# Differential attention: the second map scaled by the ratio of the sums, squared sums in the heads' norm, and another order at its end

## The reference, cut to what matters

```python
def block(qi):
    s = jnp.einsum('bqhcd,bkhcd->bhcqk', qi, k).astype(jnp.float32) * scale
    p = jax.nn.softmax(s, axis=-1)
    a = (p[:, :, 0] - lam_full * p[:, :, 1]).astype(v.dtype)
    return jnp.einsum('bhqk,bkhd->bqhd', a, v)
...
o = rms_norm(o, subln_g) * (1.0 - lambda_init)   # per head, NORM_EPS = 1e-6
return o.reshape(B, S, H * dv) @ w_o
```

## Time and profile before

| | us |
|---|---|
| median of 3 runs | 1878.87 |
| their range | 1876.99 to 1879.66 |
| the profiled execution | 1877.12 |
| its span in the trace | 1875.3 |
| first to last scores of the attention (steps 2 to 31) | 150.53 to 238.48 |

### The profile page before, as it was taken

The page is one execution under the profiler, slowest core; times in us unless marked ns, Lnnn a source line. Parts: engine busy times, 40 slices in busy tenths (PEclk is TensorE's granted clock), DMA queues, the critical chain, the costliest instruction groups (busy, mean ns, idle before and its releaser), DMA issues.

```text
span 1875.3 us, 28169 instructions
## 1 busy us (share of the span) xinstructions
PE 1845.4 (98%) x10762; PEld 1587.3 (85%) x10762; DVE 1155.8 (62%) x1647; ACT 816.0 (44%) x1433; POOL 379.4 (20%) x303
## 2 busy tenths in 40 slices
PE   9999999999999999999999999999999999999997
PEld 7885578889889899998889888897888898989897
DVE  6967956644787557677642366625474368857474
ACT  5226855434546354552123522226553455535361
POOL 0430006500032315104310033300200000522311
PEclk9999999999999999999999999999999999999999
DMA  4330014402233332423331122320451123233331
GB/s 167 124 101 23 1 56 145 147 12 91 79 102 108 95 101 90 124 68 90 92 112 56 46 90 91 99 70 30 140 180 57 58 79 103 78 115 101 99 113 45
DMA packets 99059, 167.73 MB, mean 89 GB/s; under 512 B 5632, under 2 KB 32384, under 8 KB 98688
## 3 DMA queue, kind: packets, MB, share of 16 engines
q1 hardware_dynamic: 98944, 166.15, 27.8%
HBM read 164.03 MB, written 2.10 MB: 89 GB/s over the span
## 4 chain that ended last, share of the span: by engine, by line
PE 88%; DVE 5%; ACT 3%; issue 2%; DMA 1%; SPq 0%; POOL 0%; DVEq 0%; ACTq 0%; POOLq 0%
PE ps L1953 60%; PE ps L1993 10%; PE ps L2022 6%; PE ps L2115 2%; PE ps L2302 2%; PE ps L2310 1%; PE ps L2240 1%; PE ps L2176 1%; PE ps L2170 1%; DVE small L1591 1%; DVE w_lo L1267 1%; PE ps L2249 1%; PE ps L2255 1%; PE ps L2236 1%; PE ps L2048 1%
## 5 line engine op out<-in xcount | busy, mean ns | idle before, releaser
L1267 DVE TENSOR_TENSOR w_lo<-raw,w_hi 128x1024 fp32r<-128x1024 f32 x256 | 332.5, 1322 | 238.5 <-ACT w_hi L752 236.9
L752 ACT ACTIVATE w_hi<-raw 128x1024 fp32r<-128x1024 f32 x256 | 264.6, 1057 | 345.0 <-PE ps L1953 333.5
L1953 PE MATMUL ps<-act_hi,w_lo 128*128 128x512 f32 x860 | 340.8, 396 | 2.1 <-DVE act_lo L1418 1.7
L1953 PE MATMUL ps<-act_lo,w_hi 128*128 128x512 f32 x864 | 336.7, 390 | 0.0
L1953 PE MATMUL ps<-act_hi,w_hi 128*128 128x512 f32 x860 | 335.6, 390 | 0.0
L1953 PEld LDWEIGHTS ps<-act_hi,w_lo 128*128 128x128 f32 x860 | 161.8, 188 | 39.4 <-issue 2.8
L1953 PEld LDWEIGHTS ps<-act_lo,w_hi 128*128 128x128 f32 x864 | 162.7, 188 | 34.9 <-issue 1.9
L1953 PEld LDWEIGHTS ps<-act_hi,w_hi 128*128 128x128 f32 x860 | 161.9, 188 | 34.1
L1953 PE MATMUL ps<-ff_hi,w_hi 128*128 128x512 f32 x448 | 174.4, 389 | 0.0
L1953 PE MATMUL ps<-ff_lo,w_hi 128*128 128x512 f32 x448 | 174.4, 389 | 0.0
L1953 PE MATMUL ps<-ff_hi,w_lo 128*128 128x512 f32 x448 | 174.4, 389 | 0.0
(11 more groups left out here) (252 smaller groups left out, 4043.2 us busy)
## 6 DMA issues: line engine op xcount, KB each, us to landing
raw<-in_db_w_qkv SPq DMA_DIRECT2D x72, 512.0 KB, 3.8
raw<-in_w_up SPq DMA_DIRECT2D x64, 512.0 KB, 3.8
raw<-in_w_down SPq DMA_DIRECT2D x64, 512.0 KB, 3.7
raw<-in_xa_wkv SPq DMA_DIRECT2D x32, 512.0 KB, 3.8
raw<-in_da_w_qkv SPq DMA_DIRECT2D x24, 512.0 KB, 3.9
raw<-in_xa_wq SPq DMA_DIRECT2D x16, 512.0 KB, 3.8
raw<-in_xa_wo SPq DMA_DIRECT2D x16, 512.0 KB, 3.6
raw<-in_da_w_o SPq DMA_DIRECT2D x8, 512.0 KB, 3.6
```

The lines of the kernel that those rows point to most:

```text
L752: nc.scalar.activation(w_hi[:, g % 4], raw[:, g % 4], ACT.Copy).then_inc(w_hi_ready, 1)
L1267: nc.vector.tensor_tensor(w_lo[:, g % 4], raw[:, g % 4], w_hi[:, g % 4].bitcast(f32), ALU.subtract).then_inc(w_lo_ready, 1)
L1953: last = nc.tensor.matmul(ps[:, s + m, 0:width], left, right, start=(k == 0 and n == 0 and not early), stop=(k == KT - 1 and n == 2))
```

## The change

It rewrites the weights as e1 - lambda (s1/s2) e2: the first map isn't divided. What was a pass of 128 x 512 on DVE (L1617) becomes one of 128 x 1. Each row of a head's output is then s1 times what it was, so the epsilon of the norm has to be multiplied by s1 squared: ACT writes diag(s1) squared for each step (`squared_sum`, a square of the identity matrix scaled by s1, 128 x 128), and PE adds all-ones times that, 128 x 512, to each head's statistic. Preparing pair 1 of o0 moves from steps 8 and 9 to the attention's end, pairs 2 and 3 move there too, the low parts of heads 2 to 5 are made there, and PE's pair 0 of o0 moves ahead by two transposes, a product and a statistic; the last head's statistic moves behind pair 1.

```diff
@@ scalar engine, attention()
                             nc.scalar.activation(a.p[:, n % 2, 0:a.blocks * P], a.turned_all(n),
                                                  ACT.Copy).then_inc(a.pT, 1)
+                    if a is att_d and 1 <= t <= a.n:
+                        squared_sum(a, t - 1)
...
+            def squared_sum(a, t):
+                h, s = divmod(t, a.steps)
+                if h >= 2 and s == 0:
+                    act.wait_ge(sub_stat, h - 1)
+                act.wait_ge(a.exps, 2 * t + 1)
+                nc.scalar.activation(sums_sb[:, h % 2, s * P:(s + 1) * P], ident[:, :], ACT.Square,
+                                     scale=small[:, t % 2, 4:5]).then_inc(sum_squared, 1)
+
+            def last_pairs(u):
+                def event(a, h):
+                    if h == a.heads - 1:
+                        for j in range(1, 4):
+                            heads_of(4 * u + j)
+                return event
...
             def exp_diff(a, t):
+                if t >= 2:
+                    act.wait_ge(sum_squared, t - 1)
...
-            attention(att_d, exp_diff, 2, (2, diff_out), (4, second_pair(UNITS["o0"])), (5, diff_root), (7, diff_head))
+            attention(att_d, exp_diff, 2, (2, diff_out), (5, diff_root), (7, diff_head), (-1, last_pairs(UNITS["o0"])))
...
@@ vector engine; LATE_RESTS = ((), (2, 3), (4, 5), ())
+            def last_pairs(u, heads):
+                def event(h):
+                    if h == heads - 1:
+                        for j in range(1, 4):
+                            for k in LATE_RESTS[j]:
+                                head_rest(k)
+                            rests_of(4 * u + j)
+                return event
...
-                mid(nc.vector.reciprocal(s[:, 6:8], s[:, 4:6]))
-                mid(nc.vector.tensor_scalar(e[:, S:2 * S], e[:, S:2 * S], s[:, 7:8], lam_w[:, 5:6], ALU.mult, ALU.mult))
-                nc.vector.scalar_tensor_tensor(e[:, 0:S], e[:, 0:S], s[:, 6:7], e[:, S:2 * S], ALU.mult,
+                mid(nc.vector.reciprocal(s[:, 7:8], s[:, 5:6]))
+                mid(nc.vector.tensor_scalar(s[:, 6:7], s[:, 7:8], s[:, 4:5], lam_w[:, 5:6], ALU.mult, ALU.mult))
+                nc.vector.scalar_tensor_tensor(e[:, 0:S], e[:, S:2 * S], s[:, 6:7], e[:, 0:S], ALU.mult,
                                                ALU.add).then_inc(a.probs, 1)
...
-            attention(att_d, take_max, probs_diff, range(2, att_d.n + 9), (5, second_pair(UNITS["o0"])), (6, diff_scale), (8, diff_rest))
+            attention(att_d, take_max, probs_diff, range(2, att_d.n + 9), (6, diff_scale), (8, diff_rest), (0, last_pairs(UNITS["o0"], DA_HEADS)))
...
@@ tensor engine
-                nc.tensor.matmul(ps[:, att_d.out_bank(h), :], ones[:, :], stage[:, h % 2, :], start=True,
-                                 stop=True).then_inc(sub_stat, 1)
+                pe.wait_ge(sum_squared, att_d.steps * (h + 1))
+                bank = ps[:, att_d.out_bank(h), :]
+                nc.tensor.matmul(bank, ones[:, :], stage[:, h % 2, :], start=True, stop=False)
+                nc.tensor.matmul(bank, ones[:, :], sums_sb[:, h % 2, :], start=False, stop=True).then_inc(sub_stat, 1)
...
-            attention(range(2, att_d.n + 1), *diff)
-            pe.wait_ge(att_d.exps, 2 * att_d.n)
-
-            def mixer_ends():
-                attention(range(att_d.n + 1, att_d.n + 5), *diff)
+            attention(range(2, att_d.n), *diff)
+            pe.wait_ge(att_d.exps, 2 * (att_d.n - 1))
+
+            def last_scores_read():
+                pe.wait_ge(att_d.exps, 2 * att_d.n)
+
+            def diff_ends():
+                attention(range(att_d.n, att_d.n + 4), *diff)
+
+            def last_head_stat():
+                attention(range(att_d.n + 4, att_d.n + 5), *diff)
...
+                    unit(o, act_hi, act_lo, split, late_banks=last_scores_read,
+                         before_pair={1: diff_ends, 2: last_head_stat})
```

More of the change, by code:

```diff
@@ L143 @@
 LINE_PAD = 176
+LATE_RESTS = ((), (2, 3), (4, 5), ())
 REGION = 9 * KT * 256
@@ L245, in build @@
         posf = sb("posf", [P, S])
+        with ExitStack() as scope:
+            sums_sb = sb("sums_sb", [P, 2, S], scope=scope)
         mask = sb("mask", [P, DIL, S], bf16)
@@ L360, in build @@
         sub_sq = sem("sub_sq")
+        sum_squared = sem("sum_squared")
         sub_stat = sem("sub_stat")
@@ L835, in unit, with copies @@
                         between(2 + m // 2)
-            def copies(u, dst, nb=4, width=NB, scale=None, squares_at=None, between=None, second=2, first_steps=None):
+            def copies(u, dst, nb=4, width=NB, scale=None, squares_at=None, between=None, second=2, first_steps=None, done=2):
                 def bank(m):
@@ L845, in bank @@
                                          ).then_inc(bank_out[u % 2], 4 // nb)
-                unit(u, bank, nb=nb, between=between, second=second, first_steps=first_steps)
+                unit(u, bank, nb=nb, between=between, done=done, second=second, first_steps=first_steps)
             def root(name, dst=rstd):
@@ L1032, in diff_out @@
                     act.wait_ge(sub_stat, h - 1)
-                nc.scalar.activation(stage[:, h % 2, :], ps[:, att_d.out_bank(h), :], ACT.Square).then_inc(sub_sq, 1)
+                nc.scalar.activation(stage[:, h % 2, :], ps[:, att_d.out_bank(h), :], ACT.Square,
+                                     scale=(P * EPS) ** -0.5).then_inc(sub_sq, 1)
                 nc.scalar.activation(y_sb[:, h, :], ps[:, att_d.out_bank(h), :], ACT.Copy).then_inc(a.o_out, 1)
@@ L1040, in diff_root @@
                     act.wait_ge(sub_y, h - 1)
-                nc.scalar.activation(half[:, h % 2, :], ps[:, att_d.out_bank(h), :], ACT.Ln, bias=eps[:, 0:1],
-                                     scale=1.0 / P).then_inc(sub_ln, 1)
+                nc.scalar.activation(half[:, h % 2, :], ps[:, att_d.out_bank(h), :], ACT.Ln,
+                                     scale=EPS).then_inc(sub_ln, 1)
                 act.wait_ge(sub_ln, h + 1)
@@ L1129, in mem_heads @@
                             staged_head(f"mem{layer}", k, mem_hi, MEM)
-                copies(u, lambda m: y_sb[:, m, :], squares_at=0, between=first_mem_heads)
+                copies(u, lambda m: y_sb[:, m, :], squares_at=0, between=first_mem_heads, done=2 if layer else 4)
                 copies(u + 1, lambda m: y_sb[:, 4 + m, :], squares_at=4, between=mem_heads)
@@ L1678, in diff_rest, with head_rest @@
             def diff_rest(h):
+                if h not in LATE_RESTS[1] + LATE_RESTS[2]:
+                    head_rest(h)
+            def head_rest(h):
                 rest("o0", h, act_lo[:, h, :], act_hi[:, h, :], y_sb[:, h, :])
-            attention(att_d, take_max, probs_diff, range(2, att_d.n + 9), (5, second_pair(UNITS["o0"])), (6, diff_scale), (8, diff_rest))
+            attention(att_d, take_max, probs_diff, range(2, att_d.n + 9), (6, diff_scale), (8, diff_rest), (0, last_pairs(UNITS["o0"], DA_HEADS)))
             def by_token(ap):
@@ L1741, in mem_rests @@
                         mem_tile(layer, KT)
-                unit(u, between=first_mem_rests)
+                unit(u, between=first_mem_rests, done=2 if layer else 4)
                 unit(u + 1, between=mem_rests)
@@ L2283, in _ @@
                 split = SPLITS[f"o{layer}"]
-                unit(o, act_hi, act_lo, split,
-                     before_pair={1: mixer_ends})
+                if layer == 0:
+                    unit(o, act_hi, act_lo, split, late_banks=last_scores_read,
+                         before_pair={1: diff_ends, 2: last_head_stat})
+                else:
+                    unit(o, act_hi, act_lo, split,
+                         before_pair={1: mixer_ends})
                 unit(o + 1, act_hi, act_lo, split)
```

## The result

The changed kernel is slower: 1884.38 us in the median of 7 runs (1882.85 to 1886.40) against 1878.87 of the kernel before in the same comparison, a ratio of 1.0031 with a 95% interval of 1.0021 to 1.0040. The forecast was +7.1 us; the medians differ by 5.5, the ratio says 5.8. The profiled execution took 1884.65 us, its span 1882.9.

What follows compares the result with a forecast made beforehand. A circle of waits through ACT and PE, not DVE, was taken to set the 12.24 us head period; +7.16 up to step 31's scores and -0.08 at the end gave +7.1 us, 1886.0, range 1881.0 to 1889.5.

Steps and rivals of the forecast that it cites:

- The circle through ACT and PE: Layer 0's attention: spacings between waiting instructions on ACT and PE sum to 12.24 us, the whole period of one head.
- The first rival: Attention heads: DVE is the limiter, a head would take 12.0 us, -2.4 us in all, 1876.5; chance 0.12.
- The hiding squares: Rival in the attention: ACT's squares fall into waits, circle 13.10, +3.7 us in all, 1882.6; chance 0.13.
- the dearer ones: Rival: squares at 0.40 us each add 1.4, grouped with a dearer statistic or late end, 1888.7 to 1889.5; chance 0.11.
- The circle after: One attention head after the change: 12.24 + 0.86 for PE's second product + 2 x 0.28 for squares = 13.66 us.
- 7.16 forecast: Delay of the scores of step 31: 5.16 for statistics + 3.08 for squares - 1.08 for the moved pair, in us.
- Pair 1 of o0: Steps 8 to 13 of the attention: moving its preparation out of steps 8 and 9 gives 1.08 us.
- The end: After the scores of step 31: waits -2.33, statistics +1.72, one square +0.28, number format +0.25, sum -0.08 us.
- The two statistics: Attention's end: statistics of heads 6 and 7 grow by 2 x 0.86 = 1.72 us.
- the two waits: Attention's end: step 32's transposes wait 1.06 us, the last statistic 1.27; both go, -2.33 us.
- change of number format: Attention's end: one more change between fp32 and fp32r products on PE, allowed 0.25 us, an estimate.
- pair 0 of o0+1: Behind o0: the next thing to be late, with 1.5 to 2 us of cover left before PE needs it.

Runs made afterwards that it cites:

- e5_small_pass: Kernel before with DVE's pass of 128 x 512 taken away and nothing added, old norm, no squared sums: ratio 0.9997 to the kernel before.
- e6_large_pass: Changed kernel with DVE's pass given back its size, 128 x 512 instead of 128 x 1: ratio 1.0030 to the kernel before.
- e3_no_squares: Changed kernel without ACT's squared sums, PE adding a matrix of unrelated numbers: ratio 1.0016 to the kernel before, a head 13.01 us.
- e2_maths_alone: Kernel before with the new arithmetic alone (ratio of sums, squared sums, second product), its end untouched: ratio 1.0048 to the kernel before.
- e1_end_alone: Changed kernel with the old arithmetic put back, keeping only the new order of the end: ratio 0.9975 to the kernel before.
- e4_no_product: Changed kernel without PE's second product per statistic, ACT still squaring the sums: ratio 0.9997 to the kernel before, a head 12.72 us.
- e7_gpsimd_adds: Changed kernel with squares and their addition made by GpSimd and the head's output copied by DVE: ratio 0.9977 to the kernel before.

## Why the prediction was right, point by point

*The bound.* The circle through ACT and PE held. It adds up to the whole period in both kernels, and four kernels moved it by what their edit has in it: 0.01 and 0.00 for DVE's pass taken away and given back, 0.56 for the squares, 0.85 for the product. The first rival, DVE as the limiter, fell with `e5_small_pass` and `e6_large_pass`: the head is 13.57 with either size of the pass, where that rival wanted 12.0 for the changed kernel, and stays at 12.24 when the kernel before loses the pass, where it wanted 11.7 or less. The hiding squares fell with `e3_no_squares`, the dearer ones with the spacing of 0.29.

*The circle after: 13.66 forecast, 13.57 measured.* A square cost 0.29 for 0.28, the product 0.86 for 0.86. What the sum missed is the root: the change drops the logarithm's bias, and its spacing to the exponential falls from 0.73 (212.76 to 213.49 in the trace of before) to 0.63 (231.72 to 232.35 above). I read the edit as one of numbers only. Of the 0.38 us between 7.16 forecast and 6.78 measured at the scores of step 31, 0.31 lies in the four heads from step 13 to 29 and comes of this, less the squares' 0.01.

*Pair 1 of o0: 1.08 forecast.* The kernel with the new end alone shows 1.08. In the changed kernel 18.39 us from step 8 to 13 stand against a forecast of 16.97 + 1.48 = 18.45. The sum holds there, its terms don't stand by themselves: with the new arithmetic in place the move is worth 0.17, as `e2_maths_alone` shows, and the arithmetic costs 1.59 us in these five steps with pair 1 in them (16.97 to 18.56), 2.50 without (15.89 to 18.39).

*The end: -0.08 forecast, -1.08 measured.* This is the term that was mis-sized. The two statistics were right: the changed kernel's end is 1.91 longer than that of the new end alone, forecast 2.0 (1.72 for the statistics, the square 0.19 instead of 0.28). The reordering was not: I took the two waits at their shown 1.06 and 1.27 and allowed 0.25 for a change of number format, -2.08 together; the new end alone shows 28.35 - 31.34 = -2.99. The waits that a row shows are less than what goes with them. Between the product at 240.46 and the transposes at 242.68 lie 2.22 us, though the product without a wait behind it takes 0.89 (247.70 to 248.59 above), so 1.33 went where the row said 1.06. Between the last products at 251.05 and the statistic at 254.33 lie 3.28, though those products take 1.77 without the wait (249.89 to 251.66 with the new end alone), so 1.51 went where the row said 1.27. The transposes behind the first wait stood 0.58 from the product, without it 0.44: 0.14 more. That is 2.98 of the 2.99. What is left, a further change of number format among it, adds up to nothing; no run shows the 0.25. PE at the end of the changed kernel, to hold beside the earlier trace rows:

```profile
254.89 0.60 PE L2154 MATMUL ps<-ident,e_sb 128*128 128x128 f32 x4
255.33 1.06 PE L2215 MATMUL ps<-pT_sb,v 128*128 128x128 f32 x8
256.22 1.02 PE L2225 MATMUL ps<-stage,ones 128*128 128x512 f32 x2
257.08 1.02 PE L2226 MATMUL ps<-sums_sb,ones 128*128 128x512 f32 x2
257.94 0.60 PE L2154 MATMUL ps<-ident,e_sb 128*128 128x128 f32 x4
...
265.72 1.02 PE L2225 MATMUL ps<-stage,ones 128*128 128x512 f32 x2
```

Both waits of the earlier trace rows are gone, as said. DVE and ACT finished the moved weights in time (DVE at 258.1, PE came to pair 1 at 260.1), and pair 0 of o0+1 was ready at 276.6, 1.7 us before PE came to it at 278.4; forecast were 1.5 to 2.

*The sum.* +7.1 forecast; 6.78 - 1.08 = +5.7 in the trace, 5.8 by the ratio. Both misses, 0.38 in the circle and 1.00 in the end, lie on the same side; the forecast is right without large errors that cancel.

*The rules of the Trainium skill.* The one on offloading from a saturated DVE (Perfetto Trace Analysis, Optimizing Scalar/DVE Operations) pointed at a gain. DVE was busy 94% of a head, and taking a pass off it gave 0.6 us alone and nothing in the changed kernel. The 0.41 us estimated by the Trainium skill (ScalarE: Activation LUTs, Rules for kernel authors) for 128 columns on ACT is the length that the trace shows (0.40, 0.41); what the circle pays is the spacing, 0.29. As a price of twelve squares it would have raised the sum by 12 x 0.13 = 1.6 us, where the prediction has 1.4.

## What to carry to other kernels

Before work is moved from the busiest engine to others, follow the period's own circle from instruction to instruction until the sum of the spacings is the period; only what lies in it counts. A pass off it could be dropped from the kernel before, and put back into the changed one, with a head the same to 0.01 us. When a change joins an arithmetic rewrite with a reordering, run each alone: here the reordering was worth -4.1 us and the rewrite +9.0, and since the two share a stretch they don't add up exactly. And price a wait that goes by the spacing between neighbours with and without it, not by the idle time that its row shows.

## What the runs showed of the hardware that I had not expected

**The clock fell where both kernels do the same.** In the changed kernel's profiled execution PE's granted clock was at about half from 93 to 96 us, its lower level of 1.2 GHz, in the projection ahead of the attention, where both kernels run the same instructions. PE had been busy without a pause from 80 to 92 us (12.00 of 12 us, 59 matmuls); so it had been in the kernel before (12.00, 58), whose clock stayed. The same stretch before, then after:

```profile
93.00:96.00 3.00, 3.00 (x14) 2.51 (x15) 2.96 (x4) 0.18 (x1) 1.63 (x1) 1.00 0.00 0
```

```profile
93.00:96.00 3.00, 3.00 (x8) 2.39 (x8) 2.96 (x4) 0.18 (x1) 1.95 (x1) 0.52 0.00 0
```

8 matmuls instead of 14, and 1.3 us later from there on. The traces of `e1_end_alone`, `e3_no_squares`, `e5_small_pass` and `e6_large_pass` have the same dip (a mean clock of 0.72 to 0.78 from 91 to 97 us), those of `e2_maths_alone`, `e4_no_product` and `e7_gpsimd_adds` don't (1.00), so it goes with neither part of the change. A second one, near 943 us before and 950 after, both kernels have. Whoever subtracts two spans takes the first for the change's.

**DVE slows beside GpSimd.** In the kernel with the additions on GpSimd, the same DVE instruction takes 0.75 us alone and 1.40 while GpSimd adds 128 x 512. Seven additions fall on it, and each shows this (1.40 to 1.42); where only GpSimd's pass of 128 x 128 overlaps it, by 0.2 to 0.3 us, it stays at 0.75:

```profile
212.57 0.75 DVE L1667 SCALAR_TENSOR_TENSOR e_sb<-e_sb,small 128x512 f32<-128x512 f32 x1
...
215.13 1.27 POOL L720 TENSOR_TENSOR stage<-stage,sums_sb 128x512 f32<-128x512 f32 x1 [0.82 <-ACT stage L1072]
...
215.54 1.40 DVE L1667 SCALAR_TENSOR_TENSOR e_sb<-e_sb,small 128x512 f32<-128x512 f32 x1
```
